# Running sums of a convolution in PSUM banks instead of SBUF, in one step of a hybrid decoder on Trainium2

## The reference, cut to what matters

```python
def causal_dwconv(buf, x, w):
    xp = jnp.concatenate([buf.astype(x.dtype), x], axis=1)
    ...

cv, nb_sc = causal_dwconv(bsc, cg * v, P['sc_conv'][i])        # 3 taps
yb = bg * cv
glu = ga * jax.nn.sigmoid(gg)
cc, nb_cf = causal_dwconv(bcf, glu, P['cf_conv'][i])           # 31 taps
yc = jax.nn.silu(layernorm(cc + P['cf_conv_b'][i], P['cf_ln_g'][i], P['cf_ln_b'][i]))
```

## Time and profile before

| | us |
|---|---|
| median of 3 runs | 1671.33 |
| lowest and highest run | 1669.96, 1671.79 |
| span of the profiled execution (first to last instruction) | 1668.0 |
| busy: TensorE | 1570.3 |
| busy: VectorE | 1111.6 |
| busy: ScalarE | 712.0 |
| busy: GpSimd | 681.7 |

### The profile page before, as it was taken

How to read it: one execution, slowest core, us unless ns; L and a number is a source line. 1 busy time by engine, 2 the same in 40 slices (tenths; PEclk the granted TensorE clock), 3 DMA queues, 4 the chain that set the end, 5 groups by cost and what they waited for, 6 DMA issues and landing times.

```text
span 1668.0 us, 30337 instructions
## 1 busy us (share of the span) xinstructions
PE 1570.3 (94%) x10508; PEld 1548.6 (93%) x10508; DVE 1111.6 (67%) x1580; ACT 712.0 (43%) x1053; POOL 681.7 (41%) x708
## 2 busy tenths in 40 slices
PE   6999999987999999999899999999889999999993
PEld 6999998977998999999899999898789989999993
DVE  5655437999985755535775553589998766555367
ACT  5333334424454433434643343343445544334354
POOL 2755104468321555501365540237653317553013
PEclk9999999999999999999999999999999999999996
DMA  5445433333443444532344453233344335454321
GB/s 186 168 151 188 157 126 102 127 101 127 142 145 118 149 151 150 214 139 85 108 150 144 146 197 142 97 128 126 102 143 139 131 113 179 151 185 172 121 77 57
DMA packets 52015, 230.83 MB, mean 138 GB/s; under 512 B 3408, under 2 KB 3536, under 8 KB 47568
## 3 DMA queue, kind: packets, MB, share of 16 engines
q1 hardware_dynamic: 51056, 226.60, 39.7%
q10 hardware_dynamic: 864, 3.04, 0.5%
HBM read 226.58 MB, written 3.04 MB: 138 GB/s over the span
## 4 chain that ended last, share of the span: by engine, by line
PE 70%; DVE 18%; issue 7%; ACT 2%; DMA 1%; POOL 1%; DVEq 1%; SPq 0%; POOLq 0%; ACTq 0%
PE ps L349 23%; PE ps L350 22%; PE ps L351 22%; DVE w_lo_sb L831 6%; DVE cc L984 4%; DVE ssq L843 2%; DVE x_lo L872 1%; POOL f L1330 1%; PE ps L415 1%; PE ps L423 1%; DVE ga L865 1%; DMA raw<-in_w_short 1%; DVE ga L916 1%; ACT w_hi_sb L558 1%; DMA raw<-in_w_f_up 1%
## 5 line engine op out<-in xcount | busy, mean ns | idle before, releaser
L349 PE MATMUL ps<-x_hi,w_hi_sb 128*128 128x320 f32 x2432 | 765.3, 315 | 47.8 <-DVE w_lo_sb L831 33.7
L350 PE MATMUL ps<-x_lo,w_hi_sb 128*128 128x320 f32 x2432 | 756.0, 311 | 0.0
L351 PE MATMUL ps<-x_hi,w_lo_sb 128*128 128x320 f32 x2432 | 755.8, 311 | 0.0
L831 DVE TENSOR_TENSOR w_lo_sb<-raw,w_hi_sb 128x1024 fp32r<-128x1024 f32 (+1 forms) x390 | 561.8, 1441 | 257.3 <-ACT w_hi_sb L558 256.7
L558 ACT ACTIVATE w_hi_sb<-raw 128x1024 fp32r<-128x1024 f32 (+1 forms) x396 | 438.4, 1111 | 607.0 <-PE ps L351 509.2
L349 PEld LDWEIGHTS ps<-x_hi,w_hi_sb 128*128 128x128 f32 x2432 | 460.6, 189 | 63.8 <-issue 37.5
L350 PEld LDWEIGHTS ps<-x_lo,w_hi_sb 128*128 128x128 f32 x2432 | 461.1, 190 | 0.2
L351 PEld LDWEIGHTS ps<-x_hi,w_lo_sb 128*128 128x128 f32 x2432 | 460.7, 189 | 0.0
L351 PE MATMUL ps<-mid_hi,w_lo_sb 128*128 128x320 f32 x704 | 217.4, 309 | 0.0
L349 PE MATMUL ps<-mid_hi,w_hi_sb 128*128 128x320 f32 x704 | 217.4, 309 | 0.0
L350 PE MATMUL ps<-mid_lo,w_hi_sb 128*128 128x320 f32 x704 | 217.4, 309 | 0.0
(11 more groups left out here) (142 smaller groups left out, 1397.0 us busy)
## 6 DMA issues: line engine op xcount, KB each, us to landing
raw<-in_w_f_up SPq DMA_DIRECT2D x90, 1024.0 KB, 5.3
raw<-in_w_f_dn SPq DMA_DIRECT2D x32, 1408.0 KB, 6.0
raw<-in_w_gate SPq DMA_DIRECT2D x24, 1024.0 KB, 5.3
raw<-in_w_out SPq DMA_DIRECT2D x12, 1024.0 KB, 5.3
raw<-in_w_glu SPq DMA_DIRECT2D x8, 1024.0 KB, 5.4
raw<-in_w_short SPq DMA_DIRECT2D x8, 1024.0 KB, 5.3
raw<-in_w_wo SPq DMA_DIRECT2D x8, 1024.0 KB, 5.3
raw<-in_w_pg SPq DMA_DIRECT2D x8, 1024.0 KB, 5.3
```

Source lines behind the costliest of these rows:

```text
L349: pe.matmul(out, whi, rhs_hi, start=start, stop=False, skip_group_check=True)
L350: pe.matmul(out, whi, rhs_lo, start=False, stop=False, skip_group_check=True)
L351: return pe.matmul(out, wlo, rhs_hi, start=False, stop=stop, skip_group_check=True)
L831: dve.tensor_tensor(w_lo_sb[:, j, 0:n], raw[:, j, 0:n], w_hi_sb[:, j, 0:n].bitcast(F32), ALU.subtract).then_inc(w_lo, 1)
```

## The change

The sums of the long convolution's tiles 0, 1 and 2 are kept in PSUM banks 4, 5 and 4 and those of the short convolution in bank 6. A tap reads its input from SBUF and its sum from PSUM, and writes the sum to PSUM; the last tap of each sum writes `cc` or `f` in SBUF, as before. Tile 3's one tap on VectorE stays in SBUF. Since tile 2 follows tile 0 in bank 4, its first tap waits for tile 0's last; in the short convolution, each tile's first tap waits for the last of the tile before. The pooled products go to banks 5, 6, 7 (the view `bc`) and 0.

```diff
@@ -167,7 +167,12 @@
         proj_lo = x_lo[:, :, :].rearrange("p k t -> p (k t)")[:, 0:PROJ]
         PROJ_BANKS = (4, 5, 6, 3, 2, 0, 1, 3)
         PROJ_DVE = 3
-        POOLW_BANKS = (4, 5, 6, 0)
+        POOLW_OUT = (ps[:, 5, 0:T], ps[:, 6, 0:T], bc, ps[:, 0, 0:T])
+        LONG_SUM = (ps[:, 4, 0:T], ps[:, 5, 0:T], ps[:, 4, 0:T])
+        SHORT_SUM = ps[:, 6, 0:T]
 
         loaded = sem("loaded")
         loaded_rest = sem("loaded_rest")
@@ -478,7 +483,7 @@
                         pe.wait_ge(pm_ready, L * WT + g + 1)
                         if g == 3:
                             pe.wait_ge(moved, v_moved(L, "gate1", 4))
-                        out = ps[:, POOLW_BANKS[g], 0:T]
+                        out = POOLW_OUT[g]
                         whi, wlo = pw_hi[:, g * P:(g + 1) * P], pw_lo[:, g * P:(g + 1) * P]
                         pe.matmul(out, whi, y1_hi[:, g, :], start=True, stop=False)
                         pe.matmul(out, whi, y1_lo[:, g, :], start=False, stop=False)
@@ -744,7 +749,7 @@
                     if j == 1:
                         for g in range(WT):
                             act.wait_ge(poolw_done, L * WT + g + 1)
-                            act.activation(y0_hi[:, g, :], ps[:, POOLW_BANKS[g], 0:T], ACT.Copy,
+                            act.activation(y0_hi[:, g, :], POOLW_OUT[g], ACT.Copy,
                                            scale=cur[:, COL["pool_scale"] + g:COL["pool_scale"] + g + 1]).then_inc(ya_hi, 1)
                 for j in range(4):
                     split(L, "gate2", 0, j)
@@ -973,15 +978,20 @@
                     c = COL["cf_conv"] + k * WT + t
                     if k == 0:
                         dve.wait_ge(glu_ready, L * WT + t + 1)
+                    row = cc[:, t, :]
                     for i in range(2):
-                        src, dst = part(i, cbuf, CH, t, k), tok(i, cc[:, t, :])
+                        src = part(i, cbuf, CH, t, k)
+                        before = tok(i, row if t == 3 else LONG_SUM[t])
+                        dst = tok(i, row) if k == CK - 1 else before
                         if k == 0:
                             b = COL["cf_conv_b"] + t
+                            if t == 2:
+                                dve.wait_ge(tap, L * NTAP + 2 * TAP_AT[CK - 1, 0] + i + 1)
                             dve.tensor_scalar(dst, src, cur[:, c:c + 1], cur[:, b:b + 1], ALU.mult, ALU.add).then_inc(tap, 1)
                         else:
 
                             dve.wait_ge(tap, L * NTAP + 2 * TAP_AT[k - 1, t] + i + 1)
-                            dve.scalar_tensor_tensor(dst, src, cur[:, c:c + 1], dst, ALU.mult, ALU.add).then_inc(tap, 1)
+                            dve.scalar_tensor_tensor(dst, src, cur[:, c:c + 1], before, ALU.mult, ALU.add).then_inc(tap, 1)
 
             NC3 = (2 * SK + 1) * WT
 
@@ -991,12 +1001,15 @@
                 for k in range(SK):
                     c = COL["sc_conv"] + k * WT + t
                     for i in range(2):
-                        src, dst = part(i, sbuf, SH, t, k), tok(i, f[:, t, :])
+                        src, before = part(i, sbuf, SH, t, k), tok(i, SHORT_SUM)
+                        dst = tok(i, f[:, t, :]) if k == SK - 1 else before
                         if k == 0:
+                            if t:
+                                dve.wait_ge(c3, L * NC3 + 2 * SK * (t - 1) + 2 * (SK - 1) + i + 1)
                             dve.tensor_scalar(dst, src, cur[:, c:c + 1], None, ALU.mult).then_inc(c3, 1)
                         else:
                             dve.wait_ge(c3, L * NC3 + 2 * SK * t + 2 * (k - 1) + i + 1)
-                            dve.scalar_tensor_tensor(dst, src, cur[:, c:c + 1], dst, ALU.mult, ALU.add).then_inc(c3, 1)
+                            dve.scalar_tensor_tensor(dst, src, cur[:, c:c + 1], before, ALU.mult, ALU.add).then_inc(c3, 1)
 
             def short_gate(L, t):
 
@@ -1077,7 +1090,7 @@
                         for g in range(WT):
                             dve.wait_ge(ya_hi, L * WT + g + 1)
                             c = COL["pool_scale"] + g
-                            dve.scalar_tensor_tensor(y0_lo[:, g, :], ps[:, POOLW_BANKS[g], 0:T], cur[:, c:c + 1],
+                            dve.scalar_tensor_tensor(y0_lo[:, g, :], POOLW_OUT[g], cur[:, c:c + 1],
                                                      y0_hi[:, g, :].bitcast(F32), ALU.mult, ALU.subtract).then_inc(moved, 1)
                     long_taps(L, (4, 3, 3, 3)[j])
 
```

## The result

The changed kernel takes **1618.78 us** (median of 4 runs, 1618.37 to 1620.35), against 1671.56 us before (median of 4). The ratio is 0.9695, with a 95% interval from 0.9683 to 0.9707: 52.8 us less, where 41.6 were forecast. The direction and the mechanism were right, but the time lies 3 us under the lower end of the range. The profiled execution spans 1616.9 us, 51.1 less than before.

A forecast was written before the change was run, and what follows sets the result against it. VectorE's queue was taken as the bound in one mixer stretch per layer, costing TensorE 47.6 us. Less 6 us for pile-ups, the gain is 41.6: 1668.0 - 41.6 + 3.3 = 1630 us, range 1622 to 1652.

The forecast's parts named there:

- The bound: Mixer stretch of each layer: VectorE's queue holds up TensorE, which loses 23.7 and 23.9 us, together 47.6 us.
- steps 1 and 2: Stall removed per layer: long taps 23.5 us; short convolution's later taps 1.8 us, its first taps 1.3 us.
- Step 4: Taps in the stretch: working in PSUM costs nothing extra; upper bound 0.245 us an instruction.
- the lost overlap: Rival (20%): each of 158 changed VectorE instructions a layer costs 0.08 us more, giving 1643 us.
- the stall that stays: Rival (8%): a tap's weight column counts as second SBUF operand, GpSimd still stalls it; time near 1671 us.
- the bank read and written one access at a time: Rival (12%): PSUM costs 0.245 us an instruction, making the kernel slower, about 1713 us.
- I leave 3 us a layer (an estimate): Mixer stretch: allowance for VectorE pile-ups at the short branch's gate and the output product's waits for banks; 6 us taken off.
- The pace of 0.1477 us: TensorE's time per matmul, from 325 in the 48 us behind the first stretch; 706 matmuls then take 104.3 us.
- Step 3: One layer's stretch: VectorE falls 26.6 us, from 128.0 to 101.4, below TensorE's 104.3, so TensorE becomes the bound.
- the sign of gaps on VectorE: A sign that the prediction is right: VectorE shows gaps in the two stretches.
- Step 8: GpSimd: no instruction added, removed or moved; it gets shorter since it stalls on taps too, worth nothing by itself.
- Steps 5, 6 and 7: Last tap writing SBUF, added waits between tiles' sums, and pooled products in other banks: each costs nothing.

The follow-up runs named there:

- the exchange of places: Changed kernel with the long sums of tiles 0 to 2 switching between SBUF and PSUM at every tap: 1644.45 us (0.9853).
- the writes of GpSimd: Kernel before, with GpSimd's 30 additions per layer for tile 3 replaced by two writes of zeros each: 1645.16 us (one run).
- The loads: Changed kernel with two, then four, small idle VectorE instructions after the move of each half in three phases: 1634.74 and 1662.71 us.
- the banks alone: Kernel before, with only the pooled products moved to the other PSUM banks and all sums left in SBUF: 1669.70 us (1.000).

## Why the prediction was right or wrong

- *The bound* (VectorE's queue in one stretch per layer): right. From the start of the first to the start of the last of the same 706 and 705 matmuls, the stretches took 128.7 and 128.6 us and now take 103.5 and 103.4 (25.1 and 25.2 less): 50.3 of the 51.1 us by which the profiled execution is shorter.
- *The cause and steps 1 and 2* (two SBUF operands stall beside GpSimd): right for the taps that add onto a sum, shown by the exchange of places and by the writes of GpSimd. 476 and 276 ns were measured for 474 and 276. The prediction's other half, that a single SBUF tensor does not stall, holds for the taps with a sum in PSUM and for the move, but not within SBUF for the first taps (888 ns at 64 columns beside GpSimd, 246 without); the price that step 2 gave them in PSUM was right all the same (474 and 271 ns). The Trainium skill, SBUF — State Buffer, section "Who interferes with whom", states the same: a VectorE instruction with two SBUF inputs contends with a GpSimd instruction that reads SBUF and not with one that only writes. The run with the writes agrees (473 ns beside them).
- *Step 4, the price of PSUM*: zero was right for the taps with a sum. A tap that reads and writes the same bank takes 476 ns against 474 in SBUF. The 65 ns (an estimate) that the prediction worked out from the Trainium skill, VectorE: DVE Perf Modes, section "The TRN2 errata", for an instruction that reads PSUM are not seen here either: the difference is 2 ns. By this mean, the overlap kept (six taps in 1.83 us) and the maximum of 484 ns, the rivals of the lost overlap, the stall that stays and the bank read and written one access at a time fall.
- *"I leave 3 us a layer (an estimate)"* is the step that failed: 6 us too much, the larger part of the miss. TensorE waited for nothing in the stretch, so the term is 0. The loads measure what was only felt there: the order of the work hides 2 to 3 us of VectorE's work a layer more than the change needs.
- *The pace of 0.1477 us*, read from the stretch behind, was too slow by 0.7%. The count of 325 in 48 us holds the end of TensorE's last wait for VectorE and, before and after alike, 0.2 us at the product of a norm's mean; without waits the starts are 0.1467 us apart (15 in 2.200 us; the 0.1463 above counts matmuls under way at both edges of the window). So 50.3 us were to be had, not 47.6, 2.7 more. The range's low end rested on the 47.6 as all there was, and that put the result outside.
- *What lies around the span*: the four runs after are 1.8 to 1.9 us longer than their spans. By that, the profiled execution of before (1668.0) belongs to the run of 1669.96, and the median of the four runs (1671.56) is 1.6 us above that one by scatter, not by something around the program that stays.
- Outside the stretches nothing was forecast; 0.8 us came. In the first layer, the 10 us after the mixer's last sum (502 to 512 us before, 476 to 486 after) had a granted clock of 0.83 and 41 matmuls, and now have 1.00 and 49, which gives 1.3 us over the same matmuls; 0.5 us were lost ahead of the first stretch. The second layer's fall at that place stayed (0.83 before and after). Why one went was not tested.
- Sum: 41.6 + 6 + 2.7 + 0.8 + 1.6 = 52.7 of the 52.8 us.
- *Step 3 and the sign of gaps on VectorE*: VectorE was busy for 103.2 of 104.0 us, not for 101.4, so the gaps that were to show a right prediction did not come. The short branch's product, which kept its two SBUF operands, rose from 652 to 997 ns, 1.4 us of the difference. That VectorE still came out level with TensorE and not above it was in part luck.
- *Step 8, "GpSimd gets shorter"*: wrong, without effect. Its addition for tile 3 takes 1104 ns in the stretch, 1116 before. Over the kernel before, the 34 additions that met taps and no split took 938 ns, the 26 that met a split 1306; now the 31 that meet neither split nor product take 874 and the 29 others 1347. So GpSimd lost little to the taps; it loses to the splits, which the change leaves.
- *Steps 5, 6 and 7* (last tap, waits, banks) cost nothing: the banks alone give 1.000, and no wait of VectorE on its own sums is in its waits list for the stretch.

## What to carry to other kernels

Where VectorE adds up in SBUF beside a busy GpSimd, compare the mean of an instruction with its shortest: where the excess is in forms with two SBUF operands, an idle PSUM bank for the running sum removed it here at no price, and the last addition can write SBUF directly. For a copy or a first tap, which reads one tensor, compare three prices: quiet in SBUF, stalled in SBUF, and in PSUM. Take the gain from the stretch in which that engine is the bound, at the other engine's pace in a stretch with no waits at all. Holding back 3 us a layer for pile-ups, which no row showed, was the largest error here; idle work added to the engine measures that margin. Then look for the next sum of the same kind: here it was the norms', worth another 12.4 us.

## What had not been expected of the hardware

VectorE updates a PSUM bank in place at full pace: 1.04 ns an element between the two widths, (476 - 276)/192, where SBUF has (474 - 276)/192 = 1.03. A copy of one tensor within SBUF also stalls beside GpSimd (320 ns quiet, 1000 beside it), although it has one operand, as the first taps do, and loses both its speed and its stall when it writes PSUM (480 ns).
